# Selection rounds of two score tiles moved from behind the RG-LRU loop to two places ahead of it, in a one-core hybrid encoder step

## The reference, cut to what matters

```python
s = jnp.einsum('bthd,bsd->bths', iq, ik_all)
score = jnp.einsum('bths,bth->bts', jax.nn.relu(s), iw)
score = jnp.where(adm[None], score, neg)
_, idx = lax.top_k(score, topk)          # topk = min(256, L // 4)
...
log_a = -LRU_C * r * jax.nn.softplus(-lam)
a = jnp.exp(log_a)
mult = jnp.sqrt(-jnp.expm1(2.0 * log_a))
h = associative_scan(a, mult * gi * uf)
```

## Time and profile before

| | before |
|---|---|
| median of 3 runs | 1097.14 us |
| the profiled execution: own time | 1098.84 us |
| the profiled execution: span from first to last instruction | 1097.0 us |
| PE busy | 1013.7 us (92%) |
| DVE busy | 789.3 us (72%) |
| ACT busy | 503.6 us (46%) |
| POOL busy | 352.8 us (32%) |
| mean granted TensorE clock | 0.973 |

### The profile page before, as it was taken

One profiled execution on the slowest core, in us unless ns is written; L12 is line 12 of the kernel. 1 busy time (PEld: TensorE's weight loads), 2 busy tenths in 40 slices (PEclk: granted clock), 3 DMA queues, 4 the chain that ended last, 5 costly groups with the idle time before them and its releaser, 6 DMA issues.

```text
span 1097.0 us, 15973 instructions
## 1 busy us (share of the span) xinstructions
PE 1013.7 (92%) x5658; PEld 904.6 (82%) x5658; DVE 789.3 (72%) x1469; ACT 503.6 (46%) x845; POOL 352.8 (32%) x220
## 2 busy tenths in 40 slices
PE   5989898999999999999999995988899799999995
PEld 3679886999999999999999994667777578888873
DVE  1577699999997699999999995655666325543345
ACT  4432375411222777777764224676776434111110
POOL 0222100111211455555557451345432432212120
PEclk9989999999999999999999997999999899999998
DMA  9612001222334122222223432333333327232221
GB/s 293 210 38 74 20 1 40 73 87 79 100 80 123 44 83 83 83 83 82 69 73 108 151 113 74 75 104 97 96 96 82 75 66 240 80 112 87 77 68 57
DMA packets 128277, 100.74 MB, mean 92 GB/s; under 512 B 12176, under 2 KB 119200, under 8 KB 128224
## 3 DMA queue, kind: packets, MB, share of 16 engines
q1 hardware_dynamic: 128224, 100.04, 31.2%
HBM read 74.04 MB, written 25.99 MB: 91 GB/s over the span
## 4 chain that ended last, share of the span: by engine, by line
PE 53%; DVE 23%; issue 14%; ACT 5%; DMA 2%; POOL 1%; SPq 1%; DVEq 1%; ACTq 0%; POOLq 0%
PE ps L535 16%; PE ps L536 15%; PE ps L537 15%; DVE scores L1955 7%; DVE best L1951 5%; DVE hidden L1997 2%; DVE conv L1977 2%; PE ps L1409 2%; PE ps L1671 1%; DVE scores L1916 1%; PE ps L1394 1%; ACT pt_hi L1322 1%; PE ps L1504 1%; DVE mult L1992 1%; DMA q_raw<-q_scratch 1%
## 5 line engine op out<-in xcount | busy, mean ns | idle before, releaser
L535 PE MATMUL ps<-h_hi,w_hi 128*128 128x364 f32 (+1 forms) x984 | 326.5, 332 | 4.8 <-DVE h_lo L1857 4.1
L536 PE MATMUL ps<-h_lo,w_hi 128*128 128x364 f32 (+1 forms) x984 | 325.4, 331 | 0.0
L537 PE MATMUL ps<-h_hi,w_lo 128*128 128x364 f32 (+1 forms) x984 | 325.2, 331 | 0.0
L857 POOL TENSOR_TENSOR w_lo<-w_raw,w_hi 128x1024 fp32r<-128x1024 f32 (+1 forms) x41 | 101.7, 2480 | 305.9 <-ACT w_hi L1039 305.9
L535 PEld LDWEIGHTS ps<-h_hi,w_hi 128*128 128x128 f32 (+1 forms) x984 | 185.8, 189 | 6.5 <-issue 4.2
L536 PEld LDWEIGHTS ps<-h_lo,w_hi 128*128 128x128 f32 (+1 forms) x984 | 185.6, 189 | 1.4
L537 PEld LDWEIGHTS ps<-h_hi,w_lo 128*128 128x128 f32 (+1 forms) x984 | 185.4, 188 | 0.7
L1955 DVE MATCH_REPLACE8 scores<-best,scores 128x512 f32<-128x512 f32 (+6 forms) x204 | 172.3, 855 | 0.0
L1951 DVE MAX8 best<-scores 128x8 f32<-128x512 f32 (+6 forms) x204 | 162.8, 859 | 1.8
L2110 DVE TENSOR_TENSOR pt_lo<-ps,pt_hi 128x512 fp32r<-128x512 f32 (+2 forms) x82 | 53.3, 657 | 81.4 <-ACT pt_hi L1322 81.1
L1054 ACT ACTIVATE stage<-ps 128x364 f32<-128x364 f32 (+1 forms) x66 | 29.7, 474 | 142.4 <-PE ps L537 134.5
(11 more groups left out here) (241 smaller groups left out, 1934.7 us busy)
## 6 DMA issues: line engine op xcount, KB each, us to landing
w_raw<-in_w_in SPq DMA_DIRECT2D x40, 512.0 KB, 4.3
w_mod_raw<-in_w_mod SPq DMA_DIRECT2D x8, 1024.0 KB, 12.1
y_raw<-y_scratch SPq DMA_DIRECT2D x16, 512.0 KB, 4.4
wo_raw<-in_w_out SPq DMA_DIRECT2D x10, 512.0 KB, 4.9
q_scratch<-stage SPq DMA_DIRECT2D x8, 546.0 KB, 3.7
y_scratch<-y_a SPq DMA_DIRECT2D x8, 546.0 KB, 3.6
zb_scratch<-stage SPq DMA_DIRECT2D x8, 546.0 KB, 4.0
x_in<-in_x_prompt SPq DMA_DIRECT2D x8, 512.0 KB, 8.8
```

The source lines that it names most:

```text
L535: nc.tensor.matmul(out, w_part_hi, x_hi, start=first, stop=False)
L536: nc.tensor.matmul(out, w_part_hi, x_lo, start=False, stop=False)
L537: return nc.tensor.matmul(out, w_part_lo, x_hi, start=False, stop=last)
L857: pool.tensor_tensor(w_lo[:, slot, :, 0:width], w_raw[:, slot, :, 0:width], f32(w_hi[:, slot, :, 0:width]), ALU.subtract).then_inc(w_lo_do ...
```

## The change: what it does

Three rounds of tiles 5 and 4 and one of tile 8 change their place; no instruction of the selection is added or dropped. One round of tiles 5, 4 and 8 goes directly behind the Q blocks' rounds, ahead of the clearing of `padded`. Two rounds of tiles 5 and 4 are appended to `BEFORE_LRU`. The rounds behind the loop become fewer by the same number: 5 of tile 8 where there were 6, and, between the two rounds of four tiles and `k_lo`, 2 rounds of tiles 5 and 4 where there were 5. The three rounds behind `k_lo` stay.

```diff
-BEFORE_LRU = (ROUND_ONE_TILES, (5, 4, 3, 2))
+BEHIND_Q = ((5, 4, 8),)
+BEFORE_LRU = (ROUND_ONE_TILES, (5, 4, 3, 2), (5, 4), (5, 4))
...
             with dve.Fori(0, Q_ROUNDS) as i:
                 select_round(INDEX_TILES, i * 14 + n_select)
             n_select += 14 * Q_ROUNDS
+            for tiles in BEHIND_Q:
+                select_round(tiles, n_select)
+                n_select += 2 * len(tiles)
...
-            with dve.Fori(0, SHARED_ROUNDS - Q_ROUNDS) as i:
+            shared_left = SHARED_ROUNDS - Q_ROUNDS - sum(8 in tiles for tiles in BEHIND_Q)
+            with dve.Fori(0, shared_left) as i:
                 select_round((8,), i * 2 + n_select)
-            n_select += 2 * (SHARED_ROUNDS - Q_ROUNDS)
-            left = {i: TOPK_ROUNDS - Q_ROUNDS - FIRST_ROUNDS.count(i) - sum(i in tiles for tiles in BEFORE_LRU)
+            n_select += 2 * shared_left
+            left = {i: TOPK_ROUNDS - Q_ROUNDS - FIRST_ROUNDS.count(i) - sum(i in tiles for tiles in (*BEHIND_Q, *BEFORE_LRU))
                     - KT * sum(i in tiles for tiles in (EARLY, *LATE)) for i in ROUND_ONE_TILES}
```

## The result

The changed kernel took 1088.03 us (median of 6 runs, 1085.72 to 1090.45) against 1098.25 us for the kernel before in the same session: ratio 0.991 [0.989, 0.993]. Two later sets of runs of the same changed kernel gave 1090.45 and 1090.74 us, ratios 0.9935 and 0.9937 (experiments 1 and 10).

The account below looks back on a forecast made before the run. Bound: mostly PE, which waits 9.31 us for DVE to reach the first head. Moved 12.2, lost 6.2 at k_hi, regained 1.0 at k_lo: 7.0 us off the 1097.14 median gives 1090.1 us, range 1088.5 to 1096.0.

Parts of the forecast that it names:

- How the numbers follow: Closing step on chances and range: 0.53 faster by over 0.5%, 0.45 no change, 0.02 slower; range 1088.5 to 1096.0 us.
- Moved 12.2 us: Behind the loop, three rounds of tiles 5 and 4 and one of tile 8 leave DVE: 12.2 us.
- Lost at k_hi 6.2: Ahead of k_lo, DVE arrives early and stands 6.2 us until ACT finishes k_hi, losing half of what was moved.
- k_lo to the next max 1.7 instead of 2.69: DVE's k_lo no longer meets POOL's scaling and takes 1.7 us instead of 2.69, gaining 1.0.
- DVE first: At k_lo, DVE's half starts before POOL's, so the first head comes 7.0 us earlier; chance 0.55.
- POOL first: Rival at k_lo: POOL's half goes first and DVE's is blocked; only 3.4 us gained, 1093.7 us, chance 0.30.
- PE's wait 3.8: Before the first head, PE's wait shrinks from 9.31 to 3.8 us; the clock still falls in it.
- First landing place: Round behind the Q blocks, ahead of clearing padded: ACT waits 1.3 us, covered by its later idle time; price 0.
- Second landing place: Two rounds at the loop's entry: DVE ends at 380.1, first mult could start at 380.08; price 0, conv_lo slack 1.8 us.
- Rival 4: Moved rounds not covered ahead of the loop: late entry, conv_lo outruns its slack, PE loses 10.4 us; 1100.5 us, chance 0.03.
- rival 2: Clock does not fall in PE's shorter wait, 1.5 us more gain, or DVE's stand is shorter: 1088.6 us, chance 0.06.
- rival 3: Gain given back in attention, where another wait is due at a fixed time: about 1097 us, chance 0.06.

Follow-up runs that it names:

- experiments 1 and 10: The changed kernel, unchanged, measured twice more beside the kernel before: 1090.45 and 1090.74 us, ratios 0.9935 and 0.9937.
- experiment 5: Changed kernel with the clearing of padded put back ahead of the moved round behind the Q blocks: 1089.56 us, ratio 0.9923 to the kernel before.
- experiment 3: Changed kernel with only the round behind the Q blocks moved, without the two rounds at the loop's entry: 1093.85 us, ratio 0.997 to the kernel before.
- experiment 2: Changed kernel with only the two rounds at the loop's entry moved, none behind the Q blocks: 1090.45 us, ratio 0.9937 to the kernel before.
- experiments 6, 7 and 8: The first two have their own lines; the last is the changed kernel with two rounds behind k_lo instead of three, measured again: 1086.41 us, ratio 0.9894.
- experiment 9: Changed kernel with a third round of tiles 5 and 4 ahead of the loop's first mult: 1091.94 us, ratio 0.9944 to the kernel before.
- experiment 4: Changed kernel with two rounds behind k_lo instead of three, one more ahead of it: 1086.70 us, ratio 0.99 to the kernel before.
- experiment 6: Changed kernel with two rounds behind k_lo and ACT's root ahead of the split of q: 1087.68 us, ratio 0.9898 to the kernel before.
- experiment 7: Changed kernel with both halves of k_lo on POOL, none on DVE: 1091.02 us, ratio 0.9943 to the kernel before.

## Why the prediction was right in its mechanism and wrong in its range

**The step that failed** is the low end of the range in "How the numbers follow": "from 1.6 below the forecast (the lowest of the three runs lay 1.7 under their median)". The first set's median, 1088.03, lies 0.5 under it. A spread of three runs was taken for the spread of the kernel. The 18 executions of the changed kernel reach from 1085.72 to 1092.49 us, and the medians of its three sets from 1088.03 to 1090.74. The time goes with the mean granted clock: the four executions at 0.981 took 1085.72 to 1087.81, the slowest, at 0.974, 1092.49; a line through the 18 falls by 0.73 us for each 0.001 of clock and takes their standard deviation from 1.9 to 1.0 us. The sets' mean clocks were 0.9792, 0.9780 and 0.9768, which makes 0.9 and 1.8 of the 2.4 and 2.7 us by which the first set lies lower. The rest stays unexplained. The profiled execution of before had a stretch of half clock at 331 to 335, ahead of the first moved round; that of after had none there, and k_hi came 1.56 us earlier for that alone. The forecast itself, 1090.1, is within 0.7 us of the two later sets, and the side, faster by over 0.5%, held in all three.

**The sum.** 7.0 us were predicted between k_hi and PE's resumption, 6.94 measured. Term by term:

- Moved 12.2 us: right behind the loop. From gate_cols, DVE's first instruction there, to k_lo it is 651.68 - 612.30 = 39.38 us before and, without the stand, 640.98 - 4.82 - 609.07 = 27.09 after: 12.3 less. What the sum left out is that DVE leaves the loop later: gate_cols stands 33.33 us ahead of k_hi's end before, 31.88 after, and 32.52 in experiment 5, whose entry is on time but whose loop takes DVE 0.7 us longer than before; why, was not looked for. Since DVE waits for k_hi in any case, this only shortens that wait.
- Lost at k_hi 6.2: measured 4.8, by that late exit from the loop. The stand is where the surplus goes, as predicted.
- k_lo to the next max 1.7 instead of 2.69: measured 1.75.
- DVE first: right, with a lead of 0.04 to 0.05 us in every execution in which DVE stood ready, and POOL's half stretched to 5.28 to 5.30 each time. POOL first came only where DVE was late (experiment 3), and then at the predicted price. In experiment 2 DVE came last and went first by 0.04. The thin reason for DVE first, that the loser at 948.28 had scalars to fetch, was not tried. By the rule of the Trainium skill (page "SBUF — State Buffer", section "Who interferes with whom"), whoever issues first gets the shared pair and the other is blocked: here the traces agree, with 5.29 on POOL in one order and 4.21 on DVE in the other.
- PE's wait 3.8: measured 3.94. The clock fell in it, as predicted, from 657 on, and was back in 663 to 664.

**First landing place.** The wait on ACT was put at 1.3 us and measured 2.81. The 1.3 came from an execution in which PE ran at half clock at 331 to 335, and ACT was late for that reason; the executions of experiments 6, 7 and 8 with such a stretch show 1.27, 1.33 and 1.28. The price of 0 on the path held, but not by the cover that was named alone: it also took the slack of conv_lo.

**Second landing place.** "It fits to a tenth of a microsecond" was wrong by 1.5 us: the first mult came that much late, for the reason just given. The price of 0 held because of the slack of conv_lo. It was named at 1.8 us, counted to the first matmul on conv_lo; to the group's first matmul (570.34), which is the one that waits, it was 1.65, and 0.13 of that is what PE takes behind conv_lo even when it waits. The changed kernel uses it up and pays about 0.1 us in the last step. Rival 4 (slower, from an entry 8.8 us late) was the right mechanism: experiment 9 shows it at work.

**The other rivals.** The clock that does not fall (rival 2) was not this change, but it is experiment 4, and it is worth 2.3 us there and not 1.5. Nothing shows a gain given back in attention (rival 3): PE's first product of pt_hi and v_hi for the sample (64x256) stands at 707.60 before and 696.42 after, 61.97 and 55.47 us behind k_hi (55.44 in experiments 1 and 10), so 6.5 of the 6.94 are still there.

## What to carry to other kernels

Work that is moved ahead of a wait on another engine is worth only what lies behind that wait: read first when the thing waited for is done, and cap the gain there. Before an engine is relieved further, follow the chain that ran hidden beside it (here k_lo, q_raw, q_hi, root): it lay 2.3 us under the surface, and a DVE that was ready 7 us earlier bought nothing. And a range needs the spread of many executions; one fixed pair of rows, k_hi's end and PE's resumption, gave the effect to 0.01 us where whole times scattered by several microseconds.

## What the runs showed of the hardware that was not expected

- A DVE instruction of 128x9 elements can be held until POOL's is done: 1.23 us beside POOL's q_lo (experiment 6) and 2.21 beside POOL's k_lo (experiment 7) instead of 0.17. In both it ended 0.03 to 0.04 us behind POOL's end.
- The selection's instructions are not held. In experiment 7 POOL's k_lo ran from 645.07 on beside them at 3.66 us, and they kept their times (timeline, DVE, experiment 7):

```profile
646.70 0.95 DVE L1953 MAX8 best<-scores 128x8 f32<-128x768 f32 x1
...
649.42 0.81 DVE L1957 MATCH_REPLACE8 scores<-best,scores 128x640 f32<-128x640 f32 x1
```

- The low-clock stretches around attention's start go with PE's wait for the first head. Counted between 655 and 690, PE was at 1.2 GHz for 17.1 us in the execution with a wait of 9.31, 13.7 with 7.32, 6.8 to 10.2 with 3.6 to 4.1, and 0 to 3.4 with 1.7 or less. Elsewhere, stretches come and go between executions of one kernel, and go with most of the scatter of its times.
